# Second mixer of a three-block model on one Trainium2 core: the two upper levels of the triangular inverse on 32x32 and 64x64 blocks instead of masked 128x128 matrices

## The chip, the core and the metric

One core of one Trainium2 chip (trn2) runs the whole program. The metric is the device time of one execution in microseconds (us), the median over the runs. The engines are PE (TensorE, with its weight loads shown apart as PEld), DVE (VectorE), ACT (ScalarE), POOL (GpSimd) and SP (SyncE, which issues the DMAs).

## What is computed

The program is a chain of blocks on x of 256 tokens by 1024 channels, each block a mixer and an MLP, all in fp32 accuracy. The change lies in the second mixer of the second block, `_rwkv7_mixer`, whose core is a recurrence over the tokens for each of 16 heads of 64 channels:

```python
def step(S, inp):
    r_t, w_t, k_t, v_t, kk_t, kka_t = inp
    sa = jnp.einsum('bhvk,bhk->bhv', S, -kk_t)
    S = (S * w_t[:, :, None, :] + sa[..., None] * kka_t[:, :, None, :]
         + v_t[..., None] * k_t[:, :, None, :])
    y = jnp.einsum('bhvk,bhk->bhv', S, r_t)
    return S, y
```

The kernel doesn't step over tokens. It takes 256 tokens as two chunks of 128 (CH = 2, P = 128, T = 256). Within a chunk the rows `sa` of a head solve a unit triangular system of 128 by 128 whose strict part L holds the products of keys of two tokens. The kernel needs W, the inverse of that triangular matrix, in the transposed form WT, because it is used as the stationary operand of the matmuls that solve for `sa`. There are 16 heads times 2 chunks, 32 such matrices.

## The kernel before, in words

**The inverse.** The 32x32 diagonal blocks of all 32 matrices are inverted together on DVE (a chain of products and sums, lines 1812 and 1815). Two levels follow on PE. A level merges pairs of inverted blocks of size b (level 5: b = 32; level 6: b = 64) into inverted blocks of size 2b: with L_b the part of L that lies between the two blocks of a pair, X = L_b W and then WT gets X^T WT added. `left_products` (matmul line 2512) makes X, `right_products` (line 2524) makes the addition to WT. Level 6 also needs W of level 5 and not only WT, so `turn` (line 2532) transposes the WT of level 5 on PE. All of these work on whole 128x128 matrices that are zero outside the blocks.

**The round.** The recurrence runs in four rounds q = 0..3, one for each quarter of the heads: 4 heads by 2 chunks, so 8 matrices of 128x128, kept in two PSUM banks (h = 0, 1) of 4 each. Round q prepares its inverse and three masked products of keys and receptances, and carries, with one round of delay (p = q-1), the solution, the state and the outputs of the round before. Nothing schedules this: the order on each engine is the order in which the code is written, and semaphores tie the engines. The loop of PE, `for q in range(4)`, issues

1. `left_products(q, 0)`; `pairs` K with a (line 2447, banks 6 and 7);
2. `outputs_by_channel(q-2)` (lines 2613, 2620), from q = 2 on; `right_products(q, 0)`;
3. `pairs` K with R, after DVE has masked what the first `pairs` left in banks 6 and 7; `turn(q)`;
4. `pairs` A with R, after DVE has masked the second;
5. `left_products(q, 1)`; `first_solution(p)` (lines 2551, 2557); `right_products(q, 1)`;
6. `state(p)` (2564, 2566), `first_sides(q)` (2538), `bonus_sums(q)` (2433), `second_sides(p)` (2573, 2577), `pairs` A with a for q+1, `second_solution(p)` (2585), `outputs(p)` (2593 to 2604).

All `pairs` use the same two banks 6 and 7, and each of them writes both banks to its end. So the three of a round, and the one for the next round's L, stand in line behind DVE's reading of the one before.

**DVE in a round**: `masked` AK (line 1828, two instructions), `add_level(q, 0)` (1847), `masked` RK, `gate(q-2)` from q = 2 on (1880 to 1885), `masked` RB, `bonus_products` (1737), `add_level(q, 1)`, `take_state(p)` (1852), `bonus(q)` (1745), then `take_l(q+1)` (1837, four instructions that mask L for level 5 and level 6), and from q = 1 on `statistics(p)` (1862, 1865) and `normalise(p)` (1871). In round 0 two preparations of weights, `low` (1185), stand ahead of the first `masked`. `first_solution(p)` waits for `gate(p-1)`, since it writes the banks that the gate reads. `outputs_by_channel` waits for `normalise`.

**ACT in a round**: `take_x(q, 0)` copies X from PSUM (line 1078, two instructions of 128x512), `take_w(q)` copies the transposes of `turn` (1078, two), `take_x(q, 1)` (two), the copies of `first_solution` (1114), `spread_w(q+1)` (1091, four instructions that place the 32x32 inverses on the diagonals of W), `copy_rhs0` (1124), `spread_wt(q+1)` (1091, four). 

The fp32 matmuls appear in the trace as two records of matmul and two of weight load each, so that 8 matmuls show as x16; a transpose on PE is one record.

## Time and profile before

| | |
|---|---|
| runs | 1127.13 us median of 3 (1125.69 to 1127.22) |
| the profiled execution's own time | 1125.85 us |
| its span in the profile | 1124.1 us |
| mean granted clock of TensorE | 0.986 of full speed |
| PE busy | 1075.0 us, 96% of the span |
| DVE busy | 733.0 us, 65% |
| ACT busy | 548.9 us, 49% |
| POOL busy | 41.4 us, 4% |
| the chain that ended last | PE 81%, DVE 13%, "issue" 3%, ACT 2% |

The profile is of one execution. A busy PE there means that a matmul is in flight: matmuls are pipelined and their ends are modelled, so starts are surer than ends, and the time that a group of matmuls takes is read from its start to the start of the next group. The four rounds of the second mixer lie between 798 and 893 us of the span, and the projection out of the mixer is interleaved from 893 us on.

### The profile page before, as it was taken

The page shows a single profiled execution, that of the slowest core. Times are in us where ns is not written, and L with a number is a line of the kernel's source. Part 1 is how long each engine was busy: PE and PEld are TensorE (multiplying, and loading weights), DVE is VectorE, ACT ScalarE, POOL GpSimd, SP SyncE. Part 2 cuts the span into 40 slices and gives each one's busy share as a digit, 9 for nine tenths or more (in the row PEclk, how much of TensorE's full clock was granted, in tenths as well). Part 3 has the DMA queues.
Part 4 walks back from the last instruction along what each step waited for, and adds up shares of the span by engine and source line. Part 5 has one row for each costly group of instructions (what it writes and reads, how often), then busy time and mean ns, then how long its engine had stood idle before and what let it go on. Part 6 is the DMA issues. An engine that isn't in the chain of part 4 may idle for free.

```text
span 1124.1 us, 20540 instructions
## 1 busy us (share of the span) xinstructions
PE 1075.0 (96%) x8650; PEld 1044.9 (93%) x8650; DVE 733.0 (65%) x1005; ACT 548.9 (49%) x653; POOL 41.4 (4%) x41
## 2 busy tenths in 40 slices
PE   6979999999999999999999999999599999999997
PEld 6979899999998899999999998999588999999997
DVE  5797765544468777666555568799856558445453
ACT  5554645444436455354344437894444226434341
POOL 0051000000000000000000000031000000000000
PEclk9889999999999999999999999999899999999999
DMA  9332446555753655566555536233000137655511
GB/s 313 101 113 75 139 132 218 187 187 181 291 169 117 214 186 182 161 180 203 178 187 187 187 113 187 82 127 113 1 1 1 38 113 242 192 182 174 185 73 38
DMA packets 116960, 167.19 MB, mean 149 GB/s; under 512 B 5792, under 2 KB 97568, under 8 KB 116512
## 3 DMA queue, kind: packets, MB, share of 16 engines
q1 hardware_dynamic: 115184, 165.85, 45.9%
q8 instruction: 46, 0.75, 0.3%
q10 hardware_dynamic: 1712, 0.43, 0.2%
q14 instruction: 18, 0.15, 0.0%
HBM read 165.23 MB, written 1.05 MB: 148 GB/s over the span
## 4 chain that ended last, share of the span: by engine, by line
PE 81%; DVE 13%; issue 3%; ACT 2%; DMA 1%; POOL 0%; SPq 0%; DVEq 0%; ACTq 0%; POOLq 0%
PE banks L1954 23%; PE banks L1955 23%; PE banks L1956 23%; DVE sb_w_low L1185 3%; PE banks L2447 1%; PE banks L2524 1%; DVE sb_arena L1815 1%; DVE sb_state L1812 1%; PE banks L2512 1%; ACT sb_w_high L637 1%; DMA sb_raw<-in_w_in 1%; PE banks L2038 1%; PE banks L2093 0%; PE banks L2103 0%; DVE sb_arena L1229 0%
## 5 line engine op out<-in xcount | busy, mean ns | idle before, releaser
L1185 DVE TENSOR_TENSOR sb_w_low<-sb_raw,sb_w_high 128x2048 fp32r<-128x2048 f32 x150 | 346.2, 2312 | 254.4 <-ACT sb_w_high L637 254.3
L637 ACT ACTIVATE sb_w_high<-sb_raw 128x2048 fp32r<-128x2048 f32 x150 | 285.7, 1912 | 267.5 <-PE banks L1956 263.6
L1954 PE MATMUL banks<-sb_act_high,sb_w_low 128*128 128x256 f32 x1376 | 395.0, 287 | 10.8 <-DVE sb_arena L1238 6.5
L1956 PE MATMUL banks<-sb_act_high,sb_w_high 128*128 128x256 f32 x1376 | 389.7, 283 | 0.0
L1955 PE MATMUL banks<-sb_act_low,sb_w_high 128*128 128x256 f32 x1376 | 388.8, 283 | 0.0
L1954 PEld LDWEIGHTS banks<-sb_act_high,sb_w_low 128*128 128x128 f32 x1376 | 261.4, 190 | 15.5 <-DVE sb_arena L1238 6.7
L1955 PEld LDWEIGHTS banks<-sb_act_low,sb_w_high 128*128 128x128 f32 x1376 | 260.9, 190 | 0.5 <-issue 0.2
L1956 PEld LDWEIGHTS banks<-sb_act_high,sb_w_high 128*128 128x128 f32 x1376 | 259.2, 188 | 0.0
L1955 PE MATMUL banks<-sb_hidden_low,sb_w_high 128*128 128x256 f32 x896 | 253.3, 283 | 0.0
L1954 PE MATMUL banks<-sb_hidden_high,sb_w_low 128*128 128x256 f32 x896 | 252.6, 282 | 0.7 <-DVE sb_hidden_low L1638 0.6
L1956 PE MATMUL banks<-sb_hidden_high,sb_w_high 128*128 128x256 f32 x896 | 253.1, 283 | 0.0
L1954 PEld LDWEIGHTS banks<-sb_hidden_high,sb_w_low 128*128 128x128 f32 x896 | 170.2, 190 | 1.2 <-DVE sb_hidden_low L1638 1.1
L1956 PEld LDWEIGHTS banks<-sb_hidden_high,sb_w_high 128*128 128x128 f32 x896 | 168.1, 188 | 0.0
L1955 PEld LDWEIGHTS banks<-sb_hidden_low,sb_w_high 128*128 128x128 f32 x896 | 167.9, 187 | 0.1
L1485 DVE TENSOR_TENSOR sb_hidden_low<-sb_arena,sb_hidden_high 128x512 fp32r<-128x512 f32 x48 | 31.2, 686 | 11.3 <-ACT sb_hidden_high L836 11.3
L836 ACT ACTIVATE sb_hidden_high<-sb_arena 128x512 fp32r<-128x512 f32 x48 | 27.7, 618 | 20.4 <-PE banks L1956 20.4
L1480 DVE TENSOR_TENSOR sb_arena<-sb_arena 128x512 f32<-128x512 f32 x48 | 30.7, 681 | 0.0
L2512 PE MATMUL banks<-sb_over_act 128*128 128x128 f32 x128 | 18.0, 299 | 12.3 <-DVE sb_over_act L1837 11.6
L1078 ACT ACTIVATE sb_over_act<-banks 128x512 f32<-128x512 f32 x24 | 13.6, 594 | 32.0 <-PE banks L2532 19.6
L2512 PEld LDWEIGHTS banks<-sb_over_act 128*128 128x128 f32 x128 | 16.5, 209 | 13.2 <-issue 12.7
L1954 PE MATMUL banks<-sb_w_high,sb_act_low 128*128 128x512 f32 x64 | 26.3, 410 | 0.0
L612 POOL TENSOR_SCALAR sb_arena<-sb_arena 128x256 f32<-128x256 f32 x8 | 10.3, 1299 | 425.9 <-DVE sb_act_low L1693 425.9
(350 smaller groups left out, 1138.5 us busy)
## 6 DMA issues: line engine op xcount, KB each, us to landing
sb_raw<-in_ffn_w SPq DMA_DIRECT2D x64, 1024.0 KB, 5.2
sb_raw<-in_w_up SPq DMA_DIRECT2D x16, 1024.0 KB, 5.3
sb_raw<-in_w_down SPq DMA_DIRECT2D x16, 1024.0 KB, 5.0
sb_raw<-in_sgu_w_in SPq DMA_DIRECT2D x16, 1024.0 KB, 5.4
sb_raw<-in_rwkv_w_rkv SPq DMA_DIRECT2D x12, 1024.0 KB, 5.2
sb_raw<-in_w_in SPq DMA_DIRECT2D x10, 1024.0 KB, 10.1
sb_raw<-in_sgu_w_out SPq DMA_DIRECT2D x8, 1024.0 KB, 5.0
sb_raw<-in_w_out SPq DMA_DIRECT2D x4, 1024.0 KB, 4.9
```

Of the source, the lines that this page charges most:

```text
L637: nc.scalar.activation(whi[s][:], raw[s][:], ACT.Copy).then_inc(hi_done, 1)
L836: nc.scalar.activation(hid_hi[:, 2 * s:2 * s + 2, :], FB.r[:, 2 * s:2 * s + 2, :], ACT.Square)\
L1078: nc.scalar.activation(dst[:, 4 * h:4 * h + 4, :], bank[b + h][:].rearrange("p (a b) -> p a b", a=4), ACT.Copy).then_inc(then, 1)
L1185: nc.vector.tensor_tensor(wlo[s][:], raw[s][:], f32(whi[s][:]), ALU.subtract).then_inc(lo_done, 1)
L1480: nc.vector.tensor_tensor(FB.h[:, hs, :], FB.r[:, hs, :], FB.r[:, hs, :], ALU.mult).then_inc(r_sq, 1)
L1485: nc.vector.tensor_tensor(hid_lo[:, hs, :], FB.h[:, hs, :], f32(hid_hi[:, hs, :]), ALU.subtract)\
L1812: base.add(nc.vector.tensor_tensor(tmp, RW.LB[:, j + 1:, j:j + 1].broadcast_to(shape), RW.WB[:, j:j + 1, 0:j + 1].broadcast_to(shape), ALU ...
L1815: base.add(nc.vector.tensor_tensor(RW.WB[:, j + 1:, 0:j + 1], RW.WB[:, j + 1:, 0:j + 1], tmp, ALU.add))
L1954: nc.tensor.matmul(dst, l_lo, r_hi, start=start, stop=False, **kw)
L1955: nc.tensor.matmul(dst, l_hi, r_lo, start=False, stop=False, **kw)
L1956: return nc.tensor.matmul(dst, l_hi, r_hi, start=False, stop=stop, **kw)
L2512: ins = nc.tensor.matmul(bank[h][:, n * P:n * P + P], LTl[:, 4 * h + n, :], RW.W[:, 4 * h + n, :], start=True, stop=True)
```

## The change

Level 5 and level 6 multiply only the blocks that aren't zero, on those rows and columns of the array where the blocks lie. L5, W5 and X5 are now packed with 32 columns per matrix, L6, W6 and X6 with 64. `left_products(q, 0)` becomes two matmuls of 32x32x32 for each matrix (16 in place of 8), `right_products(q, 0)` two of these and a third one, which makes the corner of W that level 6 needs (24 in place of 8), so that `turn` and its 8 transposes go. Level 6 stays at 8 matmuls on each side, of 64x64x64. DVE's masks of L (four of 128x512) become four copies of 32 partitions by 128 and two of 64 by 256; its two additions to WT of each level become four copies of 32 by 128 at level 5 and two of 64 by 256 at level 6. ACT's copies shrink likewise, and `spread_w` issues three instructions without a scale in place of four with one; `spread_wt` is as before. POOL clears a corner of W6 once, early. 

```diff
-    RW.W, RW.X, RW.L5, RW.L6 = part(0, 8), part(1024, 8), part(2048, 8), part(3072, 8)
+    small = lambda o, n: over_act[:, o:o + 8 * n].rearrange("p (a b) -> p a b", b=n)
+    RW.W5, RW.X5, RW.L5 = small(0, 32), small(256, 32), small(512, 32)
+    RW.W6, RW.X6, RW.L6 = small(1024, 64), small(1536, 64), small(2048, 64)
...
+            pool.wait_ge(w_used, U_WO)
+            pool.memset(RW.W6[0:32, :, 32:64], 0.0).then_inc(w_corner, 1)
...
             def take_x(q, l):
                 n = XD + 4 * q + 2 * l
-                halves(RW.X, 0, inv_x_ps, n, inv_x, lambda h: act.wait_ge(inv_d_ps, n + h - 1))
+                for h in range(2):
+                    act.wait_ge(inv_x_ps, n + h + 1)
+                    act.wait_ge(inv_d_ps, n + h - 1)
+                    ms = slice(4 * h, 4 * h + 4)
+                    if l == 0:
+                        dst, src = RW.X5[:, ms, :], bank[h][:, 0:P]
+                    else:
+                        dst, src = RW.X6[64:P, ms, :], bank[h][64:P, 0:T]
+                    nc.scalar.activation(dst, src.rearrange("p (a b) -> p a b", a=4), ACT.Copy).then_inc(inv_x, 1)
 
             def take_w(q):
-                halves(RW.W, 0, inv_t_ps, WD + 2 * q, inv_w)
+                for h in range(2):
+                    act.wait_ge(inv_d_ps, XD + 4 * q + h + 1)
+                    nc.scalar.activation(RW.W6[32:64, 4 * h:4 * h + 4, 0:32],
+                                         bank[2 + h][32:64, T:T + P].rearrange("p (a b) -> p a b", a=4), ACT.Copy)\
+                        .then_inc(inv_w, 1)
...
-                spread(RW.W, RW.WWB, q, wide_w)
+                w = RW.WWB[:, :, 8 * q:8 * q + 8].rearrange("p i n -> p n i")
+                nc.scalar.activation(RW.W5[:], w, ACT.Copy).then_inc(wide_w, 1)
+                for b in range(2):
+                    rows = slice(32 * b, 32 * b + 32)
+                    nc.scalar.activation(RW.W6[rows, :, rows], w[rows, :, :], ACT.Copy).then_inc(wide_w, 1)
...
-                        nc.vector.tensor_tensor(dst[:, 4 * h:4 * h + 4, :], four(bank[6 + h][:]),
-                                                over(level_mask(l), 4), ALU.mult).then_inc(l_masked, 1)
+                        src, ms = four(bank[6 + h][:]), slice(4 * h, 4 * h + 4)
+                        if l == 5:
+                            for b in (0, 64):
+                                ins = nc.vector.tensor_copy(RW.L5[b:b + 32, ms, :], src[b:b + 32, :, b + 32:b + 64])
+                        else:
+                            ins = nc.vector.tensor_copy(RW.L6[0:64, ms, :], src[0:64, :, 64:P])
+                        ins.then_inc(l_masked, 1)
...
-                    if l:
-                        dve.wait_ge(inv_t_ps, WD + 2 * q + h + 1)
-                    nc.vector.tensor_tensor(WT[:, hs, :], WT[:, hs, :], four(bank[2 + h][:]), ALU.add).then_inc(inv_wt, 1)
+                    if l == 0:
+                        for b in (0, 64):
+                            ins = nc.vector.tensor_copy(WT[b:b + 32, ms, b + 32:b + 64], four(bank[2 + h][b:b + 32, 0:P]))
+                    else:
+                        ins = nc.vector.tensor_copy(WT[0:64, ms, 64:P], four(bank[2 + h][0:64, 0:T]))
+                    ins.then_inc(inv_wt, 1)
...
                     for n in range(4):
-                        ins = nc.tensor.matmul(bank[h][:, n * P:n * P + P], LTl[:, 4 * h + n, :], RW.W[:, 4 * h + n, :],
-                                               start=True, stop=True)
+                        g = 4 * h + n
+                        if l == 0:
+                            for b in (0, 64):
+                                ins = nc.tensor.matmul(bank[h][b + 32:b + 64, 32 * n:32 * n + 32], RW.L5[b:b + 32, g, :],
+                                                       RW.W5[b:b + 32, g, :], start=True, stop=True)
+                        else:
+                            ins = nc.tensor.matmul(bank[h][64:P, 64 * n:64 * n + 64], RW.L6[0:64, g, :],
+                                                   RW.W6[0:64, g, :], start=True, stop=True)
...
                     for n in range(4):
-                        ins = nc.tensor.matmul(bank[2 + h][:, n * P:n * P + P], RW.X[:, 4 * h + n, :], WT[:, 4 * h + n, :],
-                                               start=True, stop=True)
+                        g = 4 * h + n
+                        if l == 0:
+                            for b in (0, 64):
+                                nc.tensor.matmul(bank[2 + h][b:b + 32, 32 * n:32 * n + 32], RW.X5[b + 32:b + 64, g, :],
+                                                 WT[b + 32:b + 64, g, b + 32:b + 64], start=True, stop=True)
+
+                            ins = nc.tensor.matmul(bank[2 + h][32:64, T + 32 * n:T + 32 * n + 32], WT[32:64, g, 32:64],
+                                                   RW.X5[32:64, g, :], start=True, stop=True)
+                        else:
+                            ins = nc.tensor.matmul(bank[2 + h][0:64, 64 * n:64 * n + 64], RW.X6[64:P, g, :],
+                                                   WT[64:P, g, 64:P], start=True, stop=True)
                     ins.then_inc(inv_d_ps, 1)
-            def turn(q):
-                for h in range(2):
-                    pe.wait_ge(inv_wt, WTD + 4 * q + h + 1)
-                    for n in range(4):
-                        ins = nc.tensor.transpose(bank[h][:, n * P:n * P + P], RW.WTs[q % 2][:, 4 * h + n, :], ident)
-                    ins.then_inc(inv_t_ps, 1)
...
                 pairs(q, RW.K, RW.R, (6, 7), rec_ps)
-                turn(q)
```

What PE issues in round 1 of the kernel before, from the end of `outputs_by_channel`'s place on (`right_products` of level 5, the two `pairs` with `turn` between them, level 6 around `first_solution`):

```order
L2524 MATMUL banks<-sb_raw,sb_over_act 128x128 x8
L2447 MATMUL banks<-sb_arena 128x128 x8
L2532 MATMUL banks<-sb_constants,sb_raw 128x128 x8
L2447 MATMUL banks<-sb_arena 128x128 x8
L2512 MATMUL banks<-sb_over_act 128x128 x8
L2551 MATMUL banks<-sb_arena,sb_raw 128x64 x4
L2557 MATMUL banks<-sb_constants,sb_arena 128x128 x4
L2524 MATMUL banks<-sb_raw,sb_over_act 128x128 x8
```

The same stretch of the changed kernel, whose lines 2559 and 2562 alternate eight times, then 2471 is `pairs`, 2544 and 2565 are level 6, 2585 and 2591 `first_solution`:

```order
L2559 MATMUL banks<-sb_raw,sb_over_act 32x32 x2
L2562 MATMUL banks<-sb_over_act,sb_raw 32x32
L2471 MATMUL banks<-sb_arena 128x128 x16
L2544 MATMUL banks<-sb_over_act 64x64 x8
L2585 MATMUL banks<-sb_arena,sb_raw 128x64 x4
L2591 MATMUL banks<-sb_constants,sb_arena 128x128 x4
L2565 MATMUL banks<-sb_raw,sb_over_act 64x64 x8
```

The last two `pairs` of the round now follow each other directly; nothing of PE's stands between them.

What DVE issues in round 2 before (`take_l` for it, statistics, normalise, the masks, the additions and the gate):

```order
L1837 TENSOR_TENSOR sb_over_act<-banks,sb_constants 128x512 x4
L1862 BN_STATS sb_arena<-banks 128x6 x8
L1865 BN_AGGR sb_arena<-sb_arena 128x2 x8
L1871 TENSOR_SCALAR sb_raw<-banks,sb_arena 128x64 x8
L1828 TENSOR_TENSOR sb_raw<-banks,sb_constants 128x512 x2
L1847 TENSOR_TENSOR sb_raw<-sb_raw,banks 128x512 x2
L1828 TENSOR_TENSOR sb_raw<-banks,sb_constants 128x512 x2
L1880 TENSOR_SCALAR sb_arena<-banks,sb_vectors 128x256 x2
L1883 TENSOR_TENSOR sb_arena<-sb_arena 128x512
L1885 TENSOR_TENSOR sb_arena<-sb_arena,banks 128x512
```

and in the changed kernel:

```order
L1855 COPY sb_over_act<-banks 32x128 x4
L1857 COPY sb_over_act<-banks 64x256 x2
L1886 BN_STATS sb_arena<-banks 128x6 x8
L1889 BN_AGGR sb_arena<-sb_arena 128x2 x8
L1895 TENSOR_SCALAR sb_raw<-banks,sb_arena 128x64 x8
L1843 TENSOR_TENSOR sb_raw<-banks,sb_constants 128x512 x2
L1868 COPY sb_raw<-banks 32x4x32 x4
L1843 TENSOR_TENSOR sb_raw<-banks,sb_constants 128x512 x2
L1904 TENSOR_SCALAR sb_arena<-banks,sb_vectors 128x256 x2
L1907 TENSOR_TENSOR sb_arena<-sb_arena 128x512
L1909 TENSOR_TENSOR sb_arena<-sb_arena,banks 128x512
```

Each instruction stands where it stood; only the four masks and the two additions are six and four smaller copies.

## Rows read from the trace of the kernel before

**Rows 1.** Busy time of each engine in stretches: us, busy (records), PEclk, DMA share, GB/s

```profile
798.00:800.00 2.00, 1.92 (x9) 1.95 (x10) 2.00 (x4) 1.82 (x3) 0.00 (x0) 0.50 0.00 0
820.00:841.00 21.00, 20.65 (x203) 19.64 (x199) 11.10 (x19) 9.63 (x18) 0.00 (x0) 1.00 0.01 2
```

**Rows 2.** Timeline, PE, rounds 0 and 1: start, length, records, idle before and releaser

```profile
798.08 3.75 PE L2512 MATMUL banks<-sb_over_act 128*128 128x128 f32 x16 [11.55 <-DVE sb_over_act L1837]
...
805.39 1.16 PE L2447 MATMUL banks<-sb_arena 64*128 64x128 f32 x16 [0.39 <-DVE sb_raw L1828]
806.49 1.09 PE L2532 MATMUL banks<-sb_constants,sb_raw 128*128 128x128 f32 x8
807.93 1.16 PE L2447 MATMUL banks<-sb_arena 64*128 64x128 f32 x16 [0.35 <-DVE sb_raw L1828]
809.02 2.05 PE L2512 MATMUL banks<-sb_over_act 128*128 128x128 f32 x16
810.91 2.01 PE L2524 MATMUL banks<-sb_raw,sb_over_act 128*128 128x128 f32 x16
812.76 1.00 PE L2538 MATMUL banks<-sb_arena,sb_raw 128*128 128x64 f32 x8
...
815.55 1.16 PE L2447 MATMUL banks<-sb_over_hidden,sb_arena 64*128 64x128 f32 x16 [0.87 <-DVE sb_arena L1745]
817.51 2.02 PE L2512 MATMUL banks<-sb_over_act 128*128 128x128 f32 x16 [0.79 <-issue]
819.46 1.16 PE L2447 MATMUL banks<-sb_over_hidden,sb_arena 64*128 64x128 f32 x16
...
822.53 1.16 PE L2447 MATMUL banks<-sb_arena 64*128 64x128 f32 x16
...
825.07 1.16 PE L2447 MATMUL banks<-sb_arena 64*128 64x128 f32 x16 [0.35 <-DVE sb_arena L1828]
...
829.33 1.95 PE L2524 MATMUL banks<-sb_raw,sb_over_act 128*128 128x128 f32 x16
831.12 0.39 PE L2564 MATMUL banks<-sb_arena,sb_keys_by_token 128*128 128x128 f32 x2
```

**Rows 3.** Timeline, PE, round 2

```profile
846.00 0.65 PE L2620 MATMUL banks<-sb_constants,sb_raw 128*128 128x128 f32 x4 [0.64 <-DVE sb_raw L1871]
846.49 1.95 PE L2524 MATMUL banks<-sb_raw,sb_over_act 128*128 128x128 f32 x16
...
850.90 1.16 PE L2447 MATMUL banks<-sb_arena 64*128 64x128 f32 x16 [0.35 <-DVE sb_raw L1828]
...
853.88 1.00 PE L2551 MATMUL banks<-sb_arena,sb_raw 128*128 128x64 f32 x8
...
856.95 0.39 PE L2564 MATMUL banks<-sb_arena,sb_keys_by_token 128*128 128x128 f32 x2
```

**Rows 4.** Timeline, DVE: base inverse, head of round 0, rounds 1 and 2

```profile
778.01 0.42 DVE L1815 TENSOR_TENSOR sb_arena<-sb_arena,sb_state 128x256 f32<-128x256 f32 x1
...
797.13 2.48 DVE L1837 TENSOR_TENSOR sb_over_act<-banks,sb_constants 128x512 f32<-128x512 f32 x4
...
823.73 1.29 DVE L1828 TENSOR_TENSOR sb_arena<-banks,sb_constants 128x512 f32<-128x512 f32 x2 [0.40 <-PE banks L2447]
...
850.77 0.99 DVE L1880 TENSOR_SCALAR sb_arena<-banks,sb_vectors 128x256 f32<-128x256 f32 x2
...
852.51 0.69 DVE L1885 TENSOR_TENSOR sb_arena<-sb_arena,banks 128x512 f32<-128x512 f32 x1
```

**Rows 5.** Timeline, ACT, rounds 0 and 1

```profile
811.60 2.63 ACT L1091 ACTIVATE sb_over_act<-sb_raw,sb_constants 128x256 f32<-128x256 f32 x4
...
829.09 0.39 ACT L1114 ACTIVATE sb_arena<-banks 128x256 f32<-128x256 f32 x1 [0.24 <-PE banks L2551]
829.53 0.60 ACT L1114 ACTIVATE sb_keys_by_token<-banks 128x512 f32<-128x512 f32 x1
```

**Rows 6.** One line's instructions, 2512: duration ns min/median/max

```profile
L2512 PEld LDWEIGHTS banks<-sb_over_act x128: 186/192/333, 798.1 to 879.5; 128*128 128x128 f32 x128
```

More of the change, by code:

```diff
@@ L377, in build_on @@
     RW.pz, RW.stats, RW.mv, RW.rs = (carve(16728, 8), carve(16736, 8, 6), carve(16784, 8, 2), carve(16800, 8, 1))
-    part = lambda o, n: over_act[:, o:o + n * P].rearrange("p (a b) -> p a b", b=P)
     second = lambda s, h: raw[s][:, 1024 * h:1024 * h + 1024].rearrange("p (a b) -> p a b", b=P)
-    RW.W, RW.X, RW.L5, RW.L6 = part(0, 8), part(1024, 8), part(2048, 8), part(3072, 8)
+    small = lambda o, n: over_act[:, o:o + 8 * n].rearrange("p (a b) -> p a b", b=n)
+    RW.W5, RW.X5, RW.L5 = small(0, 32), small(256, 32), small(512, 32)
+    RW.W6, RW.X6, RW.L6 = small(1024, 64), small(1536, 64), small(2048, 64)
     RW.AK, RW.RK = [second(0, 0), carve(6152, 8, P)], [second(0, 1), carve(7176, 8, P)]
@@ L423, in build_on @@
     l_masked, wide_w, wide_wt = sem("l_by_level"), sem("w_spread"), sem("wt_spread")
+    w_corner = sem("w_corner_cleared")
     a_ready, rhs_done = sem("removal_keys"), sem("first_sides")
@@ L1072, in _ @@
             values_by_token(3)
-            def halves(dst, b, done, value, then, more=lambda h: None):
-                for h in range(2):
-                    act.wait_ge(done, value + h + 1)
-                    more(h)
-                    nc.scalar.activation(dst[:, 4 * h:4 * h + 4, :], bank[b + h][:].rearrange("p (a b) -> p a b", a=4),
-                                         ACT.Copy).then_inc(then, 1)
             def take_x(q, l):
                 n = XD + 4 * q + 2 * l
-                halves(RW.X, 0, inv_x_ps, n, inv_x, lambda h: act.wait_ge(inv_d_ps, n + h - 1))
-            def take_w(q):
-                halves(RW.W, 0, inv_t_ps, WD + 2 * q, inv_w)
+                for h in range(2):
[7 more added lines that the diff above has]
+                    nc.scalar.activation(dst, src.rearrange("p (a b) -> p a b", a=4), ACT.Copy).then_inc(inv_x, 1)
+            def take_w(q):
+                for h in range(2):
[3 more added lines that the diff above has]
+                        .then_inc(inv_w, 1)
             def spread(dst, src, q, done):
@@ L1831, in take_l @@
             def take_l(q):
-                for l, dst in ((5, RW.L5), (6, RW.L6)):
+                for l in (5, 6):
                     for h in range(2):
@@ L2501, in left_products @@
             def left_products(q, l):
-                LTl = (RW.L5, RW.L6)[l]
                 if l == 0:
-                    pe.wait_ge(wide_w, q + 1)
+                    pe.wait_ge(wide_w, 3 * q + 1)
+                else:
+                    pe.wait_ge(wide_w, 3 * q + 3)
+                    pe.wait_ge(w_corner, 1)
                 for h in range(2):
@@ L2523, in right_products @@
                     for n in range(4):
-                        ins = nc.tensor.matmul(bank[2 + h][:, n * P:n * P + P], RW.X[:, 4 * h + n, :], WT[:, 4 * h + n, :],
-                                               start=True, stop=True)
-                    ins.then_inc(inv_d_ps, 1)
-            def turn(q):
-                for h in range(2):
-                    pe.wait_ge(inv_wt, WTD + 4 * q + h + 1)
-                    for n in range(4):
-                        ins = nc.tensor.transpose(bank[h][:, n * P:n * P + P], RW.WTs[q % 2][:, 4 * h + n, :], ident)
-                    ins.then_inc(inv_t_ps, 1)
+                        g = 4 * h + n
[5 more added lines that the diff above has]
+                                                   RW.X5[32:64, g, :], start=True, stop=True)
+                        else:
+                            ins = nc.tensor.matmul(bank[2 + h][0:64, 64 * n:64 * n + 64], RW.X6[64:P, g, :],
+                                                   WT[64:P, g, 64:P], start=True, stop=True)
+                    ins.then_inc(inv_d_ps, 1)
             def first_sides(q):
```

2 lines of the change are left out of this document (1 added, 1 removed).

## The prediction

> **What bounds the kernel now.** I read the busy time by stretches first, then PE's timeline through the rounds, then the timelines of DVE and ACT beside it. [rows 1] show that inside the rounds PE has a matmul in flight for 20.65 of 21 us at the full clock (granted 1.00, that is 2.4 GHz), while DVE is busy for 11.10 and ACT for 9.63. So in the rounds PE paces, and time that is taken off PE counts except where it waits for DVE in any case. Those places carry the argument, and [rows 2, 3] show them as PE's idle time: before each `pairs`, because DVE must first mask banks 6 and 7 (0.39 at 805.39, 0.35 at 807.93, 825.07 and 850.90), before `pairs` of the next L (0.87 at 815.55), before level 5 of the next round (0.79 at 817.51), and 0.64 at 846.00, where the transposes of `outputs_by_channel` wait for `normalise`.
>
> **Prices.** *A record of 128x128* is 0.112 us: 831.12 less 829.33 is 1.79 for 16 [rows 2]. *A change between row sets of the array*: level 5 takes 819.46 less 817.51, 1.95, for the same 16 records when `pairs` on 64 rows follows, so 0.16 more [rows 2]. *A record of a small block* isn't in the trace, since every weight load there has 128 columns. Lower bound: nothing, if these records run beside each other. Upper bound: 0.112, if the size doesn't matter. The 16 records of `pairs` on 64 rows, 0.068 apart (1.09 from 806.49 less 805.39, with the change of row set in it) [rows 2], lie between. I take the price in proportion to the columns that are loaded and streamed: 0.028 for 32x32x32 and 0.056 for 64x64x64. Then level 5 costs 32 records or 0.90 on the left and 48 records or 1.34 on the right, where each side was 1.79; level 6 costs 0.90 on either side instead of 1.79.
>
> The Trainium skill speaks against small blocks here. TensorEngine Tiling (Array Packing), Performance Considerations, Instruction Overhead, says that a matmul with one column takes as long as one with 60. By it a 32-column record costs about 0.025 of streaming at 2.4 GHz by itself, an estimate from that page, so that splitting further gains nothing; no row here shows it, and the sum would stay as it is.
>
> *DVE's copies*: durations are 0.42 for 256 elements and 0.69 for 512 [rows 4], so about 0.29 for 128; four instructions of 512 in 2.48 are 0.62 apart, 0.07 under the duration, so I take 0.23 for 128 and 0.36 for 256. Four plus two are 1.64 for `take_l` where it was 2.48, so 0.8 less. *ACT's copies*: 0.39 for 256 elements where it was 0.60 [rows 5]. `spread_w` goes from four to three of 0.66 (2.63 by 4) [rows 5]; it lies beside PE's work, is ready well before level 5 of the next round, and I cost its gain at nothing. POOL's memset is early on an idle engine: nothing.
>
> **Round 0.** PE has nothing in front of it but DVE. `take_l` ends 0.8 earlier, and with it the two `low` behind it, the AK mask, and the K with R `pairs` of 805.39. Level 5 has all the time from 798 to 804.6 for its work. Between 805.39 and 807.93 nothing is gained: `turn` (806.49, 1.09) [rows 2] ran while DVE did the RK mask of 1.29 [rows 4], which starts only when `pairs` ends. Without `turn` PE stands idle for 1.3 instead of 0.35. **The removed transposes thus give nothing here or in any round.** From level 6 on (809.02) there is no other work between left and right, only ACT's copy: 810.91 less 809.02 is 1.89, of which half the matmuls 0.90 and the copy 0.60, so latencies 0.39. Now 0.45 + 0.39 + 0.39 = 1.23 to the start, 0.90 of right products with their second half a little delayed by the second copy, 2.05 in all, and 0.16 to go back to 128 rows: 2.2 instead of 3.74 (812.76 less 809.02), **1.5 less**. Then from 815.55 to 819.46, 3.91 long: `pairs` 1.16 and after it all of `take_l`, 1.64, that the next `pairs` waits for, with 0.15 of latencies: 2.95, **0.95 less**; the left products, which start with L5's first two copies, end about there too. Up to 819.46: 0.8 + 1.5 + 0.95 = **3.25**.
>
> **Round 1.** From 819.46 to 822.53, 3.07: now `pairs` 1.09, right products of level 5 1.34 and 0.16 for the other row set, 2.6; the AK mask would allow 2.5. **0.5 less.** To 825.07 the same 2.54 as before. From there to `state` at 831.12, 6.05: `pairs` 1.09, left 0.90 + 0.10, `first_solution` 1.28 + 0.16, right 0.90 + 0.16, and 0.16 behind it, 4.75: **1.3 less**. ACT's copy of the keys (0.60, 829.53) is ready just before `state` then. The rest of the round has no edited part and PE paces it. Up to its end: 5.05.
>
> **Rounds 2 and 3.** The left products of level 5 give nothing: PE waits at 846.00 for `normalise`, a chain from the outputs over statistics that the change doesn't touch; the wait only grows. Then 0.49, right products 1.34 + 0.16 + 0.10, so the K with R `pairs` comes at 848.1 instead of 850.90 less 2.54, 848.36: **0.27 less**. From the A with R `pairs` (850.90, now 850.63), `pairs` 1.09, left 1.00, 0.16 bring PE to `first_solution` at 852.9; but that waits for `gate(q-2)`, which ran from 850.77 to 853.20 [rows 4] and now ends 0.27 earlier: 853.0 instead of 853.88 [rows 3]. This is the wait that takes over. `first_solution` 1.28, right 1.06, 0.16 give `state` at 855.5 instead of 856.95: **1.45 less** in round 2, and the same in round 3.
>
> **Sum**: 3.25 + 1.8 + 2 x 1.45 = 7.95, say 8.0. Behind 893 us the projection, the loads of the last MLP's weights and all else start from events of these rounds, so the gain stays. Against the profiled execution, 1125.85, that is 1117.85; the median of the runs shown is 1.28 above it, and against it I predict **1119.1 us**. What a measurement of this kernel can tell from no change is about 0.2%, 2.3 us.
>
> **Rivals.**
> *The small records overlap.* Level 5 alternates rows 0 to 31 with rows 64 to 95. For it speaks `pairs` on two sets of 64 rows, at 0.068 a record instead of 0.112 [rows 2]; against it, that those write two banks and level 5 one. Level 5 at 0.014 on the left, and 0.9 on the right, since two of three there share rows: 0.1 more in round 1 and 0.45 more in rounds 2 and 3, 1118.1. With level 6 at half of 0.056 too, 0.6 + 0.9 + 0.9 more: 1115.7. Chance 0.22. The Trainium skill, TensorEngine Tiling (Array Packing), Restrictions and Gotchas, PSUM Pressure, says that different row tiles can't use the same PSUM bank at once. By that rule level 5 stays at the forecast; no run here shows it yet.
>
> *Load and stream of a small record come one after the other*, 0.056 at level 5. Then level 5 costs 1.8 and 2.7: 1.1 later in round 0 (left and `pairs` at the half clock, then 2.7, end at 805.7), 0.4 + 1.34 in round 1, 1.34 each in rounds 2 and 3, 5.5 in all, gain 2.5: 1124.6. Against it: on 128 rows a load takes 0.19 [rows 6] and still records are 0.112 apart, so loads do run under matmuls of the same rows. Chance 0.13.
>
> *The price doesn't shrink with the block (slower).* 112 records in place of 72 at 0.112 each: the right products of level 5 take 5.4. In round 0 they begin at about 804.6 and end at 810.2 instead of 805.39, 4.8 lost and 0.3 won back; round 1 loses 1.7 on the left, 3.6 on the right and 0.5 in changes of row set; rounds 2 and 3 lose 5.0 + 0.3 each. 21 in all: 1148. It decides from where a level 5 record costs more than about 0.066: 208 of them lie on the path then (48 on the right in each of four rounds and half of the 32 on the left in round 1), and 0.038 more for each eats the 8. Chance 0.08.
>
> *The clock.* It is at half (0.50, 1.2 GHz) at 798 after PE's idle time, and at full by round 1 [rows 1]. If it rises one stretch of 4 us later, 1 to 1.5 is lost; if PE's longer waits keep it down through the rest of round 0, most of the gain goes: about 1125. Chance 0.07. Forecast and what lies close to it: 0.50.
>
> **Numbers.** The range goes from overlap at both levels, 1115.5, to serial load and stream with a little more, 1125.5. It leaves out the price that doesn't shrink and a part of the clock case. Faster by over 0.2% has the forecast, overlap and part of the two cases between: 0.82. Within 0.2%: 0.08. Slower: 0.10.
>
> **What would show it.** Level 5 left from its start to the next `pairs` about 1.1, right about 1.5; idle time of PE of 1.3 between the last two `pairs` in every round; a wait of `first_solution` for the gate's line in rounds 2 and 3; over 1 us of wait for `normalise` before the transposes; `take_l` in 1.6. The forecast is wrong if level 5's right products take over 2.7, if the granted clock is 0.50 after 804, or if `state` of round 1 follows its A with R `pairs` by over 5.5.

## The result and the profile after

The changed kernel is slower: 1145.41 us median of 4 runs (1136.63 to 1146.78) against 1126.41 us before, a ratio of 1.0153 with a 95% interval of 1.0109 to 1.0197. The prediction was 1119.1 us, faster, with a range to 1125.5.

The profile's page of the changed kernel, its busy time and its row of the granted clock in 40 slices, shows PE in flight for 9 us more than before and DVE and ACT for less:

```profile
PE 1084.0 (95%) x8810; PEld 1050.1 (92%) x8810; DVE 727.7 (64%) x1021; ACT 539.0 (47%) x649; POOL 43.9 (4%) x42
...
PEclk9889999999999999999999999998577799999999
```

What differs is the clock in the slices of the second mixer, 5 and 7 tenths. The busy time by stretches of the changed kernel (the columns are those of [rows 1]) gives it more exactly:

```profile
798.00:820.00 22.00, 16.94 (x186) 14.97 (x188) 12.75 (x21) 8.24 (x17) 0.00 (x0) 0.50 0.01 1
820.00:840.00 20.00, 17.42 (x187) 15.52 (x186) 8.42 (x20) 4.50 (x11) 0.00 (x0) 0.50 0.00 1
840.00:860.00 20.00, 16.92 (x205) 15.19 (x204) 10.56 (x41) 5.15 (x13) 0.00 (x0) 0.84 0.01 2
860.00:880.00 20.00, 19.85 (x135) 18.51 (x136) 8.38 (x20) 6.03 (x13) 0.00 (x0) 0.62 0.01 1
880.00:900.00 20.00, 16.77 (x203) 14.79 (x202) 12.58 (x42) 4.24 (x12) 0.00 (x0) 0.72 0.00 1
900.00:920.00 20.00, 19.53 (x145) 19.03 (x144) 5.50 (x27) 4.19 (x12) 0.00 (x0) 0.85 0.18 53
```

Before, the clock was at half (0.50, 1.2 GHz) when round 0 began, behind 11.5 us in which PE stood idle, came up at 802 us and stayed at full (1.00, 2.4 GHz) to the end of the rounds [rows 1, 2]. Now it comes up only at 844 us. Read in stretches of 1 us, it then falls again at 858, is back at 875, falls once more at 889 and is back at 905. As it has two levels, 0.50 and 1.00, a stretch's mean tells how long it was at half: twice what is missing to 1, times the length. Over the six stretches that is 22 + 20 + 6.4 + 15.2 + 11.2 + 6.0, 81 us.

The four rounds can be measured by themselves, from the first record of `left_products` in round 0 to the first of the last `first_solution`, for behind that point nothing differs: from there to the end of the span all kernels of this case take 231.7 to 231.8 us (before, 1124.1 less 892.33 is 231.8). Ahead of it the code is the same but for a small memset and, in some runs below, filler. Before, the two records stand at 798.08 [rows 2] and at 892.33 in PE's timeline:

```profile
892.33 0.39 PE L2551 MATMUL banks<-sb_arena,sb_raw 128*128 128x64 f32 x2
```

so the rounds took 94.25 us. PE's timeline of the changed kernel, with some of its rows in rounds 0, 1 and 2 and that last point:

```profile
798.07 1.07 PE L2541 MATMUL banks<-sb_over_act 32*32 32x32 f32 x32 [11.49 <-DVE sb_over_act L1855]
799.23 2.08 PE L2471 MATMUL banks<-sb_over_hidden,sb_arena 64*128 64x128 f32 x16
...
804.95 2.08 PE L2471 MATMUL banks<-sb_arena 64*128 64x128 f32 x16 [2.65 <-DVE sb_raw L1843]
808.41 2.08 PE L2471 MATMUL banks<-sb_arena 64*128 64x128 f32 x16 [1.38 <-DVE sb_raw L1843]
810.41 1.86 PE L2544 MATMUL banks<-sb_over_act 64*64 64x64 f32 x15
...
829.56 2.08 PE L2471 MATMUL banks<-sb_arena 64*128 64x128 f32 x16 [1.37 <-DVE sb_arena L1843]
831.57 1.96 PE L2544 MATMUL banks<-sb_over_act 64*64 64x64 f32 x16
833.46 1.97 PE L2585 MATMUL banks<-sb_arena,sb_raw 128*128 128x64 f32 x8
...
851.38 0.69 PE L2541 MATMUL banks<-sb_over_act 32*32 32x32 f32 x32
852.01 1.16 PE L2471 MATMUL banks<-sb_over_hidden,sb_arena 64*128 64x128 f32 x16
...
856.09 0.66 PE L2654 MATMUL banks<-sb_constants,sb_raw 128*128 128x128 f32 x4 [1.86 <-DVE sb_raw L1895]
856.68 0.22 PE L2559 MATMUL banks<-sb_raw,sb_over_act 32*32 32x32 f32 x2
...
857.31 1.47 PE L2471 MATMUL banks<-sb_arena 64*128 64x128 f32 x16
...
912.05 0.50 PE L2585 MATMUL banks<-sb_arena,sb_raw 128*128 128x64 f32 x3
```

The rounds take 113.98 us, 19.7 more. The lines to set beside [rows 2] are those of `pairs`: 16 records from 808.41 to 810.41 are 2.00, where they were 1.09 from 807.93 to 809.02. Unedited work takes up to twice its time: `first_solution`'s four small products from 833.46 are on their way for 1.97 instead of 1.00 [rows 3]. The waits for DVE's masks that the prediction named are there, 1.38 and 1.37 between the last two `pairs`, and 1.86 for `normalise`. And the small matmuls are cheap. At the full clock, in round 2, level 5 takes 0.63 on the left (851.38 to 852.01) and 0.63 on the right (856.68 to 857.31).

So the edits made PE's own work shorter, and the clock got worse. The experiments ask whether the one brings about the other, whether that is the whole of it, and which part of the edit does it.

### The profile page after: what moved, and what is told of

The parts are those of the page before. It is cut to its first block, busy times and chain, and to the rows that moved or that the text cites. A ratio compares the mean times of both kernels' runs of the same rounds, so it can differ in the third digit from the quotient of the medians.

```text
span 1143.8 us, 20869 instructions
## 1 busy us (share of the span) xinstructions
PE 1084.0 (95%) x8810; PEld 1050.1 (92%) x8810; DVE 727.7 (64%) x1021; ACT 539.0 (47%) x649; POOL 43.9 (4%) x42
## 4 chain that ended last, share of the span: by engine, by line
PE 79%; DVE 13%; issue 3%; ACT 2%; DMA 1%; SPq 0%; POOL 0%; DVEq 0%; ACTq 0%; POOLq 0%
PE banks L1978 22%; PE banks L1979 22%; PE banks L1980 22%; DVE sb_w_low L1200 3%; PE banks L2471 2%; DMA sb_raw<-in_w_in 1%; DVE sb_arena L1830 1%; DVE sb_state L1827 1%; ACT sb_w_high L642 1%; DVE sb_arena L1244 1%; PE banks L2544 1%; PE banks L2565 1%; PE banks L2457 1%; PE banks L2572 1%; PE banks L2585 1%
## 5 line engine op out<-in xcount | busy, mean ns | idle before, releaser
L1980 PE MATMUL banks<-sb_w_high,sb_act_high 128*128 128x512 f32 x64 | 25.4, 396 | 0.0
L1979 PE MATMUL banks<-sb_w_low,sb_act_high 128*128 128x512 f32 x64 | 25.3, 396 | 0.0
L2471 PE MATMUL banks<-sb_arena 64*128 64x128 f32 x128 | 15.3, 410 | 8.5 <-DVE sb_raw L1843 5.4
```

Of the source, the lines that this page charges most:

```text
L1979: nc.tensor.matmul(dst, l_hi, r_lo, start=False, stop=False, **kw)
L1980: return nc.tensor.matmul(dst, l_hi, r_hi, start=False, stop=stop, **kw)
L2471: ins = nc.tensor.matmul(bank[banks[e]][:, o:o + P], left[es, 2 * q + t, ms], right[es, 2 * q + t, ms], start=True, stop=True)
```

## The experiments

All times of a kernel are medians; the ratios are against the kernel before on the same chip, with 95% intervals. "Rounds" and "at half" are of the one profiled run, for the rounds alone, from the row shown or, where none is, from the same view; with a clock of two digits the time at half is good to about 1 us. A filler is work for PE that nothing reads.

Where the clock goes up and down within the rounds, the runs of one kernel spread wide: 1136.63 to 1146.78 us for the changed kernel, 1135.79 to 1149.48 for fill_small, 1139.63 to 1148.77 for fill_rows32. Medians of these kernels that lie 5 us apart can't be told from each other.

| kernel | us | ratio | rounds, us | at half, us |
|---|---|---|---|---|
| before | 1126.41 | 1 | 94.25 | 4 |
| changed | 1145.41 | 1.0153 [1.0109, 1.0197] | 113.98 | 80 |
| fill_turn | 1122.60 | 0.9970 [0.9956, 0.9984] | 91.72 | 26 |
| fill_small | 1149.20 | 1.0170 [1.0107, 1.0233] | 118.05 | 83 |
| no_turn | 1127.30 | 1.0011 [1.0001, 1.0021] | 94.37 | 6 |
| fill_all | 1118.97 | 0.9936 [0.9919, 0.9952] | 87.84 | 7 |
| level6_small | 1121.88 | 0.9956 [0.9940, 0.9973] | 89.77 | 5 |
| level5_small | 1132.82 | 1.0056 [1.0039, 1.0073] | 100.59 | 32 |
| fill_rows32 | 1140.50 | 1.0143 [1.0100, 1.0186] | 110.03 | 66 |
| fill_cols32 | 1125.60 | 0.9989 [0.9977, 1.0001] | 93.91 | 30 |
| fill_full | 1125.60 | 0.9995 [0.9985, 1.0005] | 94.19 | 28 |
| before_filled | 1127.22 | 1.0009 [1.0000, 1.0018] | 95.56 | 4 |
| level6_filled | 1122.00 | 0.9960 [0.9946, 0.9973] | 90.39 | 4 |
| fill_more | 1118.43 | 0.9926 [0.9911, 0.9940] | 85.83 | 0 |

### Fill the gap that turn left: fill_turn

```diff
+            def filler(n=8):
+                for i in range(n):
+                    nc.tensor.transpose(bank[i % 2][:, 256:256 + P], ident, ident)
...
                 pairs(q, RW.K, RW.R, (6, 7), rec_ps)
+                filler()
                 pe.wait_ge(rec_sb, rec_at(q, "RK", 1))
```

> The changed kernel with eight transposes of the constant identity between the last two pairs of each round, where turn stood; nobody reads them, they wait for nothing, and they fill some 1.0 of the 1.37 us in which PE stands idle there. Theory I (PE's idle time in the rounds lets the granted clock fall): the clock is at full from 802 or 806 on, as before the change, the half clock in the rounds shrinks from 89 us to under 15, and the time is 1117 to 1121 us. Theory S (the small blocks themselves count too little for the clock, with or without idle time): at least 40 us at half clock remain, 1130 us or more.

Measured: 1122.60 us, 1.6 above Theory I's range and far below Theory S's. (The 89 us of the expectation count from 790 on, with the idle time ahead of round 0 in them; in the rounds it is 80.) Eight transposes of a constant per round, which compute nothing, take 23 us off the changed kernel. The rounds of fill_turn in one stretch:

```profile
798.89:890.61 91.72, 82.05 (x1012) 74.11 (x1013) 54.50 (x148) 30.02 (x70) 0.00 (x0) 0.86 0.04 13
```

The clock is 0.86, so 26 us at half remain, between what the two theories said. The clock depends on what PE does in the rounds, and more work in the gaps brings it up; but idle time in this one place is not all of it.

### The same gap, filled with small blocks: fill_small

```diff
+            def filler(n=48):
+                for i in range(n):
+                    b = 64 * (i % 2)
+                    nc.tensor.matmul(bank[0][b + 32:b + 64, 256:288], ident[b:b + 32, 0:32], ident[b:b + 32, 0:32],
+                                     start=True, stop=True)
```

> As the one with eight transposes, but the filler is 48 matmuls of 32x32x32 (96 records, about 1.0 to 1.2 us at the full clock). Theory I, with any busy PE counting: the same time as with the transposes, 1117 to 1121 us. Theory S (how much of the array a matmul uses counts): the small filler does nothing for the clock, over 40 us at half clock, 1135 to 1148 us as in the changed kernel.

Measured: 1149.20 us, as Theory S said, but 1 us above the upper end of its range. The filler itself lasted 2.7 us at the half clock and so was longer than the gap of 1.4, which adds some 1.2 us in a round. The rounds of fill_small in one stretch:

```profile
797.38:915.43 118.05, 109.02 (x1365) 99.89 (x1365) 54.92 (x148) 29.94 (x70) 0.00 (x0) 0.65 0.04 11
```

PE was in flight for 109.02 of 118.05 us, 92%, against 82.05 of 91.72, 89%, in fill_turn, and had 1365 records against 1012. Yet the clock is 0.65 against 0.86. Busy time in the profile is not what tells the two apart.

### The gap without the small blocks: no_turn

```diff
-                halves(RW.W, 0, inv_t_ps, WD + 2 * q, inv_w)
+                halves(RW.W, 2, inv_wt, WTD + 4 * q, inv_w)
...
-                turn(q)
```

> The kernel before, all its matrices 128x128, with turn alone left out: take_w copies level 5's addition from its banks after DVE has added it, so that W lacks the transposition and the results of level 6 on are not the inverse. PE then stands idle for 1.3 us between the last two pairs. Theory I, if these gaps alone are enough: stretches at half clock after 806 and 1135 us or more. Theory S: the clock stays full from 802 on and the time is 1126 to 1127 us, for the wait of pairs for DVE's masks sets that place with or without turn.

This kernel leaves out the transposition: level 6 gets what DVE added at level 5, untransposed, so its results aren't the inverse, while the other instructions and their sizes stay. Measured: 1127.30 us, 0.1% above before. The rounds:

```profile
797.96:892.33 94.37, 85.45 (x788) 80.34 (x789) 60.07 (x133) 39.03 (x73) 0.00 (x0) 0.97 0.04 12
```

PE is in flight for 85.45 us instead of 89.0, and neither the clock (0.97, 0.98 before) nor the length of the rounds changes. That settles two steps: taking `turn` away gives nothing by itself, as predicted, and the 1.37 us of idle time that it leaves between the last two `pairs` do not bring the clock down while the blocks are 128x128: it is 1.00 from 804 on. It takes both, or the small blocks alone.

### Fill all of PE's waits: fill_all

```diff
+            filler(84, (4, 5))
             for q in range(4):
                 p = q - 1
                 left_products(q, 0)
...
                 right_products(q, 0)
+                if q == 0:
+                    filler(30, (4, 5))
...
+                if p < 2:
+                    filler(14, (4, 4))
```

The last is in `outputs_by_channel`, ahead of the gates; the 8 transposes of fill_turn are in it too.

> The changed kernel with transposes of the identity wherever PE stood idle: 84 of them in the 11 us ahead of round 0, 30 in round 0 behind the right products of level 5, 8 between the last two pairs of each round, 14 ahead of the gates in rounds 2 and 3. Theory I: clock 1.00 from before 798 to the end of the rounds, all edits' gain realised, 1116 to 1119 us, since round 0's stretch at half clock goes too. Theory S: half clock remains within the rounds, 1125 us or more.

Measured: 1118.97 us, a ratio of 0.9936. With the clock up, the kernel is what the prediction had drawn. PE's timeline of fill_all in rounds 0 to 2:

```profile
816.47 2.08 PE L2471 MATMUL banks<-sb_over_hidden,sb_arena 64*128 64x128 f32 x16 [0.34 <-DVE sb_over_act L1857]
819.92 2.08 PE L2471 MATMUL banks<-sb_arena 64*128 64x128 f32 x16 [0.38 <-DVE sb_arena L1843]
...
824.64 1.14 PE L2544 MATMUL banks<-sb_over_act 64*64 64x64 f32 x16
825.71 1.11 PE L2589 MATMUL banks<-sb_arena,sb_raw 128*128 128x64 f32 x8
...
843.25 0.66 PE L2660 MATMUL banks<-sb_constants,sb_raw 128*128 128x128 f32 x4 [0.38 <-DVE sb_raw L1895]
...
849.45 1.08 PE L2589 MATMUL banks<-sb_arena,sb_raw 128*128 128x64 f32 x8 [0.21 <-DVE sb_arena L1909]
```

The last row is the wait that the prediction said would take over: `first_solution` (2589) for the gate (1909) in round 2. Level 6 on the left takes 1.07 (824.64 to 825.71). One stretch at half clock is left, in round 1, where two `pairs` show 2.08 instead of 1.16. The clock fell there, between 816 and 817 us, although PE had stood idle for no more than 0.87 us at a time since round 0 began. So this fall isn't due to one long wait; ahead of it lie small blocks of both levels and several short waits.

### Which level: level6_small and level5_small

level6_small is the kernel before with level 6 on small blocks; `turn` and level 5 stay on 128x128. level5_small is the changed kernel with level 6 taken back. The left products of level6_small against the kernel before (its right products, copies and masks change likewise):

```diff
-                        ins = nc.tensor.matmul(bank[h][:, n * P:n * P + P], LTl[:, 4 * h + n, :], RW.W[:, 4 * h + n, :],
-                                               start=True, stop=True)
+                        if l == 0:
+                            ins = nc.tensor.matmul(bank[h][:, n * P:n * P + P], LTl[:, 4 * h + n, :],
+                                                   RW.W[:, 4 * h + n, :], start=True, stop=True)
+                        else:
+                            ins = nc.tensor.matmul(bank[h][64:P, 64 * n:64 * n + 64], RW.L6[0:64, 4 * h + n, :],
+                                                   RW.W[0:64, 4 * h + n, 0:64], start=True, stop=True)
...
```

> The kernel before with level 6 alone on 64x64 blocks (8 matmuls a side, their copies and masks shrunk); level 5 and turn as before. Area theory (the clock falls because the blocks leave too much of the array unused over too long a stretch): four fifths of PE's time in the rounds is unchanged, the clock stays full from 802 or 805 on, and the matmul time saved counts: 1.5 us in round 0 from the shorter way from left over the copy to right, 1.3 in round 1, and 0.9 to 1.4 in rounds 2 and 3, where gate holds first_solution: 1120 to 1122 us. If even the 64x64 blocks of level 6 are enough to bring it down: half clock within the rounds and 1126 us or more.

> The changed kernel with level 6 back on 128x128 (masks, copies, additions too); level 5 on 32x32 blocks, no turn. Area theory: of the 72 records of level 5, left, right and turn, that took some 4.7 us of each round, 1.2 us of tiny matmuls and idle time are left, so this is where most of the clock goes: 30 us or more at half clock in the rounds and 1130 us or more. If both levels are needed for the fall: clock full from 806 on and 1121 to 1124 us.

Measured: 1121.88 us with level 6 alone, in the expected range and faster than both kernels of this case, without any filler; 1132.82 us with level 5 alone, slower than before. The rounds of level6_small:

```profile
799.33:889.10 89.77, 84.50 (x821) 77.53 (x821) 55.66 (x133) 36.85 (x73) 0.00 (x0) 0.97 0.04 13
```

and of level5_small:

```profile
798.24:898.83 100.59, 84.43 (x981) 78.40 (x981) 59.03 (x148) 35.04 (x76) 0.00 (x0) 0.84 0.04 12
```

Both have PE in flight for nearly the same 84.4 us, but one is at half clock for 5 us, all of them at the start of round 0 as before, and the other for 32. Level 5, with the tiny blocks and without `turn`, is the part that costs the clock; level 6 on top of it takes the time at half from 32 to 80 us. (The 72 records in the second expectation are those of both levels; level 5 and `turn` have 40, and these are what took its 4.7 us.)

### What the filler must be: fill_rows32, fill_cols32, fill_full

Five matmuls in the gap, 10 records in all, that stream 128 columns and take nearly the same time (at the half clock of round 0, 2.43, 2.27 and 2.43 us to the next `pairs`); what differs is the part of the array. One line of each:

```diff
... fill_rows32
+                    nc.tensor.matmul(bank[i % 2][:, 256:256 + P], ident[0:32, :], ident[0:32, :], start=True, stop=True)
... fill_cols32
+                    nc.tensor.matmul(bank[i % 2][0:32, 256:256 + P], ident[:, 0:32], ident, start=True, stop=True)
... fill_full
+                    nc.tensor.matmul(bank[i % 2][:, 256:256 + P], ident, ident, start=True, stop=True)
```

> The changed kernel with five matmuls on 32 rows by 128 columns, streaming 128 columns (10 records, 1.1 us), in the gap between the last two pairs. They take the time that the eight transposes took but a quarter of the rows. If the clock follows busy time: as with the transposes, 1121 to 1125 us. If it follows rows in use: as without a filler, 1136 to 1148 us. If it follows only columns: as with the transposes.

> The same with five matmuls on 128 rows by 32 columns of weights, streaming 128 columns (10 records, 1.1 us). If the clock follows busy time or rows in use: 1121 to 1125 us. If it follows the columns in use: 1136 to 1148 us, with 70 us or more at half clock.

> The changed kernel with five matmuls of 128 rows by 128 columns, streaming 128 columns, in the gap between the last two pairs: the full-size counterpart of the two quarter-size fillers. By the theory that rows in use count and columns don't: the same as with 128 rows by 32 columns and with the transposes, 1121 to 1126 us, against the 1140 of 32 rows by 128 columns.

Measured: 1140.50 us (1139.63 to 1148.77) with 32 rows, 1125.60 us (1121.84 to 1126.74) with 32 columns, 1125.60 us (1123.59 to 1127.34) with all of both; the second is 0.6 above its expected range, the others lie in theirs. The rounds of fill_rows32:

```profile
797.54:907.57 110.03, 100.74 (x1020) 91.57 (x1021) 54.81 (x148) 29.90 (x70) 0.00 (x0) 0.70 0.04 11
```

of fill_cols32:

```profile
797.78:891.69 93.91, 84.41 (x1021) 75.17 (x1021) 54.62 (x148) 29.99 (x70) 0.00 (x0) 0.84 0.04 13
```

and of fill_full:

```profile
797.69:891.88 94.19, 84.73 (x1021) 77.11 (x1021) 54.66 (x148) 30.08 (x70) 0.00 (x0) 0.85 0.04 13
```

A quarter of the columns is as good as all of them. A quarter of the rows leaves the clock at 0.70, near the 0.65 of the changed kernel, and the ranges of the two kernels' times overlap, so that this filler isn't shown to help at all. The one clear difference between a filler that helps and one that doesn't is how many rows of the array it works on. A filler on 64 rows was not tried. The transposes of fill_turn have a median 3 us lower (1122.60), but the ranges overlap (1120.64 to 1124.63) and the profiled runs are 1.1 apart. They are 8 records instead of 10, and ten records last 2.4 us at the half clock, 1 us more than the gap, so a longer delay of the next `pairs` may be a reason; it was not tried.

### Is it the filler's gain: before_filled, level6_filled, fill_more

```diff
+            filler(84, (4, 5))
...
+                if p < 2:
+                    filler(4, (4, 4))
```

> The kernel before with the same filler in the places where it stands idle too: 84 transposes ahead of round 0 and 4 ahead of the gates in rounds 2 and 3. It asks how much of what the filled kernels gain is the change's and how much the filler's alone. By the theory that the half clock at the start of round 0 costs nothing, since there DVE's two preparations of weights set the time: 1125 to 1127 us, no change. If the half clock from 792 to 802 did cost: up to 2 us less.

> The version with level 6 alone on small blocks and the same filler, 84 ahead of round 0 and 4 ahead of the gates. Its clock was full from 804.5 on without a filler, and the 1.4 us that its first pairs came late in round 0 are what there is to get: 1120 to 1122 us.

Measured: 1127.22 and 1122.00 us, no gain for either over the same kernel without a filler; the first is 0.1% slower than before. But the filler did not hold the clock there. It was 1.00 through the start of round 0 and then fell behind the first wait for DVE's masks, in before_filled from 807.2 to 810.6 and in level6_filled from 806.4 to 809.8 (read in stretches of 0.5 us), so that the time at half was moved and not removed. PE's timeline of before_filled:

```profile
805.79 1.16 PE L2447 MATMUL banks<-sb_arena 64*128 64x128 f32 x16 [2.38 <-DVE sb_raw L1828]
806.88 1.73 PE L2532 MATMUL banks<-sb_constants,sb_raw 128*128 128x128 f32 x8
808.54 2.08 PE L2447 MATMUL banks<-sb_arena 64*128 64x128 f32 x16
```

In before_filled no block is small, and PE's waits between the filler and the fall are 0.74 and 2.38 us; in level6_filled they are 0.76 and 1.83 us, ahead of its first small block. So waits among full-size matmuls can be enough for a fall. Idle time and matmuls on few rows thus both cost the clock, and no run separates how they add. A kernel before whose clock is at full throughout was not run, so these two runs don't prove that all the gain of the filled kernels is the change's. What speaks for it is that before, the 4 us at half end ahead of a wait for DVE in any case (0.39 at 805.39 [rows 2]) and so have little to give.

fill_more is fill_all with 34 instead of 30 transposes behind the first right products, and with

```diff
+                if q == 0:
+                    filler(6, (4, 5))
                 if q < 3:
...
                     pairs(q + 1, RW.A, RW.a, (6, 7), pair_ps)
+                if q == 0:
+                    filler(4, (4, 5))
```

> The changed kernel filled everywhere as before, and now also in its waits at the end of round 0: 6 transposes before the pairs of the next L and 4 behind them, and 34 instead of 30 behind the first right products. The one stretch at half clock that was left, 816.4 to 823.2, cost some 3 us. If the theory holds that PE must have enough rows at work, it goes: clock 1.00 throughout the rounds, 1114.5 to 1117 us. If the small level 5 of round 1 by itself brings the clock down: as with the first set of fillers, 1118 to 1120 us.

Measured: 1118.43 us (1117.48 to 1118.61), ratio 0.9926, 1.4 above the upper end of what was expected from a full clock, and by its time alone within the 1118 to 1120 of the rival. The clock decides between them, and it did what the theory said:

```profile
799.05:884.88 85.83, 80.71 (x1084) 73.22 (x1085) 54.67 (x148) 30.18 (x71) 0.00 (x0) 1.00 0.05 14
```

It is 1.00 throughout, and the rounds are 2.0 us shorter than in fill_all. The span isn't: it was 1117.1 us there and is 1116.6 here, because round 0 began at 799.05 instead of 797.47. That difference of 1.6 us arises before the rounds, in code that both share, and its cause isn't known; the start lay between 797.4 and 799.3 in the profiles of this case. This version has the lowest median of those run, though its range and fill_all's (1117.05 to 1119.52) overlap.

## Why the prediction was wrong

**The step that failed is the clock.** The sum was made at the full clock's prices for everything behind round 0. The prediction had seen the half clock at 798 and weighed it as the last rival, at 0.07 and at most "about 1125", for "PE's longer waits" within round 0. In fact the clock was at half for 80 us of the rounds instead of 4, in rounds 1, 2 and 3 as well. With the clock held up by filler (fill_more) the rounds take 85.83 us, 8.4 less than before; as changed they take 113.98. So the half clock cost about 28.1 us over 80 us, 0.35 us for each and not the full half, which fits that DVE's work takes the same time at either clock (a mask 1.29 us in both) and PE waits for part of it. The prediction asked only whether the clock would come up in round 0. It never asked whether the work that is left would hold it in the other rounds, and took time off PE as a pure gain. The edit turned an even load of 128-row matmuls in levels 5 and 6 into short bursts on 32 and 64 rows and into waits; neither waits of 1.37 us with full-size blocks (no_turn) nor the small blocks with PE's waits filled (fill_more) cost the clock, while both together did, at level 5 above all. Two of the signs that the prediction named for its being wrong came true: the granted clock was 0.50 after 804, and `state` of round 1 came 8.55 us behind its A with R `pairs` (838.11 less 829.56).

**What was right.** The sum of 8.0 at the full clock, near enough, and in part by luck: fill_more's rounds are 8.4 shorter, but its parts are off in both directions and make up for each other. They are, from one `first_solution` to the next: up to the first 3.7 less (forecast 4.5, with part of round 1 in it), to the second 2.1 less (1.45), to the third 2.1 less (1.45), to the last 0.45 less (0.57). That the removed transposes give nothing: no_turn, 94.37 against 94.25. The idle time of 1.3 between the last two `pairs` (1.38 and 1.37), the wait of over 1 us for `normalise` (1.86), the wait of `first_solution` for the gate (0.21).

**Sizes that were off**, in both directions. Level 5's records: 0.63 for 32 with the change of row set in it, and 0.63 for 48, so 0.020 and 0.013 a record instead of 0.028. The rival of overlapping records was right on that, and the gain it gave in rounds 2 and 3, 0.65 more than forecast in each, is more than the 0.45 that it had priced. Both figures lie below the 0.025 that the prediction estimated for a record of 32 columns too. Level 6: 1.07 a side in place of 0.90 and a change of row set, 1.0 to 1.06, right. DVE's copies, in the timeline of the changed kernel:

```profile
797.20 1.19 DVE L1855 COPY sb_over_act<-banks 32x128 f32<-32x128 f32 x4
798.42 0.75 DVE L1857 COPY sb_over_act<-banks 64x256 f32<-64x256 f32 x2
```

0.30 each for 128 elements instead of 0.23, so that `take_l` is 1.9 and not 1.64, against 2.48 before [rows 4]; this is part of what is missing in rounds 0 and 1.

**The rule on PSUM banks** of the Trainium skill, TensorEngine Tiling (Array Packing), Restrictions and Gotchas, PSUM Pressure, that different row tiles can't use the same bank at once, did not bind as the prediction used it: level 5's left products write one bank from two sets of rows at 0.020 a record or less, below the 0.028 that the prediction had put down for records that follow each other. Whether they truly overlap or a small record is just cheaper than its columns suggest was not tried, so the rule itself isn't refuted.

**The rival that ended slower**, a price that does not shrink with the block, was wrong: its 1148 us are near the measured 1145 by coincidence, for the loss has another reason. Only the rows of the trace tell the two apart, since the small records cost a fifth of what it had supposed or less.

## What to carry to other kernels

Before PE's work is cut in a stretch where the clock is at full, ask what keeps it there: here a saving of 8.4 us turned into a loss of 19 because matmuls on 128 rows became matmuls on 32 and 64 rows and waits, and the profile's page showed it in one row, the granted clock. Try first to cut the level whose blocks keep more rows at work (here level 6 alone was 4 us faster, with nothing else needed), and try a few full-height matmuls on constants in PE's waits before giving the larger cut up (1118.4 us with fill_more). Read a saving off the chain of waits: the transposes that were removed lay beside DVE's masks and gave nothing.

## What the runs showed of the hardware

- In the changed kernel the granted clock, at half behind 11.5 us of idle time, did not come up in the first 46 us of the rounds, though PE never stood idle for more than 2.65 us at a time; before, it came up 4 us after the rounds began. It then fell twice more, with waits of at most 1.86 us. In fill_all it fell behind waits of at most 0.87 us, with small blocks between them. Four waits of 1.37 or 1.38 with 128x128 blocks (no_turn) left it at 1.00, and one of 2.38 among such blocks (before_filled) was followed by 3 us at half.
- By the Trainium skill, TensorE: Matmul & The Clock Gate, Why this matters for your kernels, one avoids the loss of the clock by leaving no long idle gap between bursts of matmuls. Closing a gap wasn't enough here: fill_small left none between the last two `pairs` and had its clock at 0.65, as the changed kernel with its gaps of 1.4 us; the wait of 2.64 in round 0 and two of 1.9 were still there. All gaps of these rounds are shorter than the one that this section warns of, and in fill_all, with none over 0.87, the clock still fell once.
- Five matmuls on 128 rows by 32 columns did as much for the clock as five on 128 by 128 (0.84 and 0.85); five on 32 rows by 128 columns did little (0.70, without a filler 0.65).
- Transposes on PE held the clock as well: in fill_more the 84 fp32 transposes ahead of round 0 were all that PE did from 788 to 799 us, and it was 1.00 in that stretch; in the kernel before, with PE idle there, it was at half from 792 on. The Trainium skill, TensorE: Matmul & The Clock Gate, Part 4: PE-mode transpose, says that they don't count as work for the clock in the same way; these runs don't bear that out.
- A 32x32x32 record costs 0.013 to 0.020 us at the full clock where the row sets alternate, and a 64x64x64 record 0.067 (1.07 for 16 with the change of row set in it).
